# The first gatings of the next block ahead of the last GELU, a first block led by products, and one group's parts moved into it

## The reference

```python
q = (xb @ wq).reshape(PEER_BLOCK, PEER_HEADS, 2, PEER_DKEY // 2)
s = jnp.einsum('thpd,hpkd->thpk', q, keys).astype(jnp.float32)
s1, i1 = lax.top_k(s[:, :, 0], PEER_TOPK)
s2, i2 = lax.top_k(s[:, :, 1], PEER_TOPK)
cand = (s1[..., :, None] + s2[..., None, :]).reshape(PEER_BLOCK, PEER_HEADS, PEER_TOPK * PEER_TOPK)
sc, ic = lax.top_k(cand, PEER_TOPK)
e1 = jnp.take_along_axis(i1, ic // PEER_TOPK, axis=-1)
e2 = jnp.take_along_axis(i2, ic % PEER_TOPK, axis=-1)
idx = e1 * PEER_NKEYS + e2
gate = jax.nn.softmax(sc, axis=-1)
act = jax.nn.gelu(jnp.einsum('td,thkd->thk', xb, u[idx]).astype(jnp.float32), approximate=False)
return jnp.einsum('thk,thkd->td', (gate * act).astype(xb.dtype), v[idx])
```

## Time and profile before

| | |
|---|---|
| median of the three timed runs | 4544.8 us |
| their lowest and highest | 4538.14, 4556.12 us |
| the profiled execution | 4532.34 us |
| its span | 4530.7 us |
| its mean granted clock of TensorE | 0.962 |
| TensorE busy with matmuls | 4237.4 us (94%) |
| VectorE, ScalarE, GpSimd busy | 3187.9 (70%), 1437.9 (32%), 1553.5 us (34%) |

### The profile page before, as it was taken

One profiled execution on the slowest core, in us unless ns is written; L12 is line 12 of the kernel. 1 busy time (PEld: TensorE's weight loads), 2 busy tenths in 40 slices (PEclk: granted clock), 3 DMA queues, 4 the chain that ended last, 5 costly groups with the idle time before them and its releaser, 6 DMA issues. The chain is left out here.

```text
span 4530.7 us, 85734 instructions
## 1 busy us (share of the span) xinstructions
PE 4237.4 (94%) x32575; PEld 3842.7 (85%) x32575; DVE 3187.9 (70%) x6005; ACT 1437.9 (32%) x2183; POOL 1553.5 (34%) x1316
## 2 busy tenths in 40 slices
PE   7999998998668979999999998899999999999997
PEld 4898887887546878878878887899999999999996
DVE  5621434553844237899985554999999999999997
ACT  2311222111634222233346665222222222222223
POOL 6333333653031200044442222443434444343431
PEclk9999999998868989999999999999999999999998
DMA  4665674553543311134434444999999999999994
GB/s 170 209 212 186 211 244 158 193 215 122 145 130 93 131 72 38 38 131 143 145 120 165 165 165 188 334 303 298 303 300 300 300 301 302 300 302 298 302 302 158
DMA packets 523006, 928.01 MB, mean 205 GB/s; under 512 B 284032, under 2 KB 351232, under 8 KB 518688
## 3 DMA queue, kind: packets, MB, share of 16 engines
q1 hardware_dynamic: 387024, 549.29, 37.0%
q0 software_dynamic: 80960, 346.96, 22.3%
q10 hardware_dynamic: 54816, 28.85, 2.2%
HBM read 785.79 MB, written 206.30 MB: 219 GB/s over the span
## 5 line engine op out<-in xcount | busy, mean ns | idle before, releaser
L3239 POOL DMA_INDIRECT ex_rows<-expert_rows,ex_here x512 | 589.4, 1151 | 948.4 <-DVE acc_tok L3374 858.7
L3374 DVE SCALAR_TENSOR_TENSOR acc_tok<-ex_rows,ex_wsp,acc_tok 128x1024 f32<-128x1024 f32 x512 | 633.6, 1278 | 0.0
L2637 PE MATMUL ex_psa<-x_dense_high,eg_u_high 128*128 128x288 f32 x2048 | 604.2, 295 | 13.9 <-DVEq L3428 13.9
L2728 POOL TENSOR_TENSOR eg_u_low<-eg_u,eg_u_high 128x1024 fp32r<-128x1024 f32 x130 | 325.3, 2503 | 847.2 <-ACT eg_u_high L2723 847.2
L2637 PE MATMUL ex_psa<-x_dense_low,eg_u_high 128*128 128x288 f32 x2048 | 604.4, 295 | 0.0
L2637 PE MATMUL ex_psa<-x_dense_high,eg_u_low 128*128 128x288 f32 x2048 | 604.0, 295 | 0.0
L3271 PE MATMUL ex_pso<-ex_w_high,ex_v_high 128*128 128x288 f32 x2048 | 441.0, 297 | 11.0 <-DVE acc L3356 9.1
L3302 ACT ACTIVATE ex_w<-ex_psa 128x288 f32<-128x288 f32 x256 | 105.4, 412 | 1055.6 <-PE ex_psa L2637 1055.6
L3271 PE MATMUL ex_pso<-ex_w_high,ex_v_low 128*128 128x288 f32 x2048 | 439.8, 296 | 0.0
L3271 PE MATMUL ex_pso<-ex_w_low,ex_v_high 128*128 128x288 f32 x2048 | 438.4, 296 | 0.0
L3356 DVE TENSOR_TENSOR acc<-ex_pso,acc 128x576 f32<-128x576 f32 x512 | 373.8, 750 | 47.2 <-PE ex_pso L3271 47.2
(11 more groups left out here) (528 smaller groups left out, 9565.8 us busy)
## 6 DMA issues: line engine op xcount, KB each, us to landing
eg_u<-in_u SPq DMA_DIRECT2D x256, 512.0 KB, 5.2
expert_rows<-in_v SPq DMA_DIRECT2D x128, 512.0 KB, 6.9
ex_v<-in_v SPq DMA_DIRECT2D x128, 512.0 KB, 6.5
weights<-wt_stage SPq DMA_DIRECT2D x9, 4096.0 KB, 12.1
ex_g<-weights SPq DMA_DIRECT2D x128, 288.0 KB, 6.9
expert_rows<-eg_act SPq DMA_DIRECT2D x256, 128.0 KB, 1.7
proj<-in_out POOLq DMA_DIRECT2D x50, 548.5 KB, 6.5
in_w<-in_w_in SPq DMA_DIRECT2D x50, 512.0 KB, 4.7
```

The source lines that it names most:

```text
L2637: yield nc.tensor.matmul(out[:, 0:b - a], w[:, kc, :], half[:, kc, a:b], start=n == 0, stop=n == len(passes) - 1)
L2728: self.k.nc.gpsimd.tensor_tensor(self.ul[par][:, :, :], self.u[par % 2][:, :, :], self.uh[par][:, :, :].bitcast(F32), ALU.subtract).then_i ...
L3239: pool.indirect_dma_start(rows[i][:, :], None, table, index(here[par][:, t, j:j + 1]), element_offset=ROW_RUNS[t][0]).then_inc(s_row[i], 16)
L3374: v.scalar_tensor_tensor(out=acc_tok[:, t, :], in0=rows[i][:, at:at + D], scalar=wsp[:, i:i + 1], in1=acc_tok[:, t, :], op0=ALU.mult, op1= ...
```

## The change

There are four edits. In `phase_topk`, GpSimd and ScalarE leave out the parts of group 77 (the one behind group 73, `TOPK_EARLY - 1`). In `phase_spread` they make them: ScalarE the high part as its first instruction, GpSimd the low part behind the iota. In `phase_spread` TensorE takes its 18 product matmuls ahead of each batch in block 0 and, as before, behind each batch in the others. And ScalarE's gating becomes a function `gate`: the gating of batch 0 of block 0 is made ahead of the blocks, and that of batch 0 of each other block between the copy of batch 7 of the block before and that block's last GELU.

```diff
@@ phase_topk, gpsimd
                     for g, par, _ in groups:
-                        early.low(pool, g + RING, par)
+                        if not isinstance(g, int) or g < TOPK_EARLY - 1:
+                            early.low(pool, g + RING, par)
@@ phase_topk, scalar
-                        early.gelu_then_high(act, g, par, number)
+                        early.gelu(act, g, par, number)
+                        if not isinstance(g, int) or g < TOPK_EARLY - 1:
+                            early.high(act, g + RING, par, number + 1)
@@ phase_spread
+        late = TOPK_EARLY - 1 + early.RING
+        late_group = (late, late % ERING, late // ERING)
@@ gpsimd
                 nc.gpsimd.tensor_copy(iota[:, :], iota_i).then_inc(s_io, 1)
+                early.low(pool, *late_group[:2])
@@ tensor
                     for n in range(NB):
+                        if b == 0:
+                            for _ in range(FILL):
+                                next(u_steps)
                         pe.wait_ge(OH.sem, OH.now(batches[n], b))
...
                         mm.then_inc(*PE.inc(batches[n]))
-                        for _ in range(FILL):
-                            next(u_steps)
+                        if b:
+                            for _ in range(FILL):
+                                next(u_steps)
@@ scalar
+                def gate(b, n):
+                    act.wait_ge(OH.sem, OH.now(batches[n], b))
+                    for t in range(n * BATCH, n * BATCH + HALF):
+                        o_ = one2[:, t % RING, :]
+                        last = nc.scalar.activation(o_, o_, ACT.Copy, scale=selT[:, 2, TB * b + t:TB * b + t + 1])
+                    last.then_inc(*GA.inc(batches[n]))
...
                     for n in range(NB):
-                        act.wait_ge(OH.sem, OH.now(batches[n], b))
-                        for t in range(n * BATCH, n * BATCH + HALF):
-                            o_ = one2[:, t % RING, :]
-                            last = nc.scalar.activation(o_, o_, ACT.Copy, scale=selT[:, 2, TB * b + t:TB * b + t + 1])
-                        last.then_inc(*GA.inc(batches[n]))
                         if n:
+                            gate(b, n)
                             evac(n - 1)
                         if n in FINISHED:
                             early.gelu_then_high(act, *group(r, slot, FINISHED[n]))
                     evac(NB - 1)
+                    if b + 1 < NTB:
+                        gate(b + 1, 0)
                     early.gelu_then_high(act, *group(r, slot, SG_ - 1))
+
+                early.high(act, *late_group)
+                gate(0, 0)
                 in_line(body)
```

## The result

The changed kernel takes 4518.2 us (median of 14 runs, 4500.3 to 4530.1) beside 4552.5 us of the kernel before (14 runs, 4530.1 to 4559.3). The ratio is 0.9937 with a 95% interval of 0.9924 to 0.9949: 29 us faster, between 23 and 35; the two medians, 34 us apart, lie at the upper end of that. I had forecast 39.2 us, a ratio of 0.9914. The time lies in the stated range and the sign holds; the size of the largest term does not.

What follows compares the result with a forecast made beforehand. The phase was taken as bound by TensorE, except at nine places bound by ScalarE's order. Terms 32.4 + 0.5 + 6.3 = 39.2 us off the median 4544.8 gave 4505.6, predicted as 4505, range 4488 to 4522.

Steps and rivals of the forecast that it cites:

- Boundaries 2 to 8: Block boundaries after the first: the earlier gating removes TensorE's 3.0 us idle pieces and the clock falls behind them, 32.4 us.
- Next late at the boundary is nothing before TensorE itself: At a block boundary, once the gating is early: nothing else holds TensorE up, so the full 32.4 us are won.
- Boundary 0 to 1: Where blocks 0 and 1 meet: copy and gating stay uncovered, 5.4 us against 5.9 now, 0.5 us won (-0.7 to 2.2).
- The clock piece: Behind the pause between blocks 0 and 1: TensorE's lower clock costs 1.8 us, from 0.1 to 2.94.
- The start: Start of phase_spread: group 77's late parts and products ahead of batch 0 win 6.3 us, bounds 4.0 to 8.6.
- The collision of low part and one-hots: Start of phase_spread: GpSimd's low part holds up VectorE's first one-hots, a delay of 2.1 us.
- Rival A: At block boundaries: idle pieces go but the clock still falls for another reason; 27 us won, 4518 us, chance 4%.
- Rival B: At block boundaries: batch 0's gating comes a microsecond too late; 4526 us, chance 5%.
- C: At block boundaries: ScalarE waits for batch 0's one-hots ahead of the last GELU, so slower; 4563 us, chance 3%.
- D: Behind the phase: it ends earlier and the experts' phase gives the gain back; 4545 us, chance 2%.

Runs made afterwards that it cites:

- load_first: Changed kernel with SyncE's load of u moved from right behind the block table's 4 MB store to right ahead; last transposes to last GELU 434.4 us, ratio 0.9895.
- high_behind_gate: Changed kernel with ScalarE's high part that waits for u moved behind batch 3's gating, blocks 1 to 8; last transposes to last GELU 434.5 us.

## Why the prediction was right and wrong

- **Boundaries 2 to 8, 32.4 us: wrong by 8.7.** The step that failed is the sentence "Next late at the boundary is nothing before TensorE itself", with the one that no instruction of SyncE changes place. The wait ahead of batch 0 did go in every one of these blocks and the gating was in time, as worked out. What is late next lies three batches on, in a transfer: SyncE's order is the same, but the 4.5 us a boundary used to lose were the time in which the load behind the 4 MB store landed. Shown by load_first (434.4), and from the other side by high_behind_gate (434.5), both against 443.1. The term of 32.4 us measured 23.7. The forecast checked that the groups' parts are ready for TensorE, four groups ahead, and they were. It didn't check that the maker of those parts, ScalarE, blocks its own next gating while it waits.
- **Boundary 0 to 1, 0.5 us: 2.5.** The mechanism and the pause were right (3.3 us idle against 3.65). The clock piece, put at 1.8, was 0.05 in this profile and 1.7 in the second: most of the 2.0 us over the forecast's term is luck. With it the sum of 39.2 less 8.7 plus 2.0 gives the 32.5 found.
- **The start, 6.3 us: 6.3.** The collision of low part and one-hots was there with its 2.2 us. As in the sum (2353 against 2352.7), the one-hots and their gating ended last and not the products, by 0.8 us in one profile and 2.4 in the other.
- **Rival A** (clock falls for another reason): refuted; in the changed kernel two windows in blocks 2 and 5 and the whole way from batch 0 of block 1 to the last GELU (columns as in the earlier trace rows) have a grant of 1.00:

```profile
2474.00:2523.00 49.00, 47.74 (x275) 41.34 (x274) 29.88 (x48) 33.79 (x52) 14.86 (x6) 1.00 0.51 183
2620.00:2668.00 48.00, 47.15 (x272) 40.94 (x271) 29.83 (x48) 33.52 (x52) 14.87 (x6) 1.00 0.52 187
2426.29:2813.70 387.41, 380.74 (x2176) 329.95 (x2176) 231.93 (x372) 268.17 (x411) 116.55 (x47) 1.00 0.50 182
```

- **Rival B** had the right kind, a gating late by about 1 us, at the wrong one: batch 0's was in time, batch 3's wasn't. **C** and **D** are refuted by the timeline and by the 1711.9 us behind the phase.
- **The size of the whole.** The stretch of the first profile of the kernel before was 2.8 us longer than that of the second, by the clock's chance alone, so the 32.4 us of the first pair flatter the change: the means give 30.8 and the timed runs 29, against the 39.2 of the forecast.

## What to carry to other kernels

When a stall at a boundary is taken out, list every transfer that was issued during or just before it, above all one behind a large store, and ask which engine waits for it in order and what stands behind that wait. The small waits of engines off the path show where this will bite: here ScalarE waited six times for u, 0.6 to 2.1 us, and each of these waits grew by 4.4 to 5.7 us when some 4.5 us went at the boundary ahead of it. The first 4.9 us of such a wait were free, the rest TensorE paid. And compare two profiles by the stretch that the change touches: here the spans differ by 5 us while the stretch differs by 32.

## What the hardware did unexpectedly

After equal pauses of TensorE of 2.84 us the granted clock fell or didn't: in 23 of them, in three profiles, the batch behind it came 0.1 us later than the 5.91 of full clock six times and 1.5 to 2.9 us later the other seventeen. The pause of 3.1 us between blocks 0 and 1 cost 0.1 us or less in four profiles and 1.5 and 1.7 us in two, and one of 1.96 us cost 1.7. A load of 512 KB issued 1.0 us behind a store of 4 MB landed 13.8 us after its issue (12.5 to 14.6 over eight blocks), and 13.5 us (10.9 to 13.5) on another queue than the store's; issued 0.65 us ahead of the store it landed after 4.4 us (4.2 to 5.0).
